# Down projections of six feed-forward stages: some block pairs by seven products in place of eight

## The reference

```python
def swiglu(x, w_in, w_out):                 # first block, D_FF = 4096
    gate, up = jnp.split(x @ w_in, 2, axis=-1)
    return (jax.nn.silu(gate) * up) @ w_out

x = layer_norm(alpha * x + 0.5 * swiglu(x, w_ff1_in[l], w_ff1_out[l]), ln1_g[l], ln1_b[l])
x = layer_norm(alpha * x + mix, ln2_g[l], ln2_b[l])
x = layer_norm(alpha * x + 0.5 * swiglu(x, w_ff2_in[l], w_ff2_out[l]), ln3_g[l], ln3_b[l])

def swiglu_2(h, wg, wu, wd):                # second block, D_FF_2 = 2816
    return (jax.nn.silu(h @ wg) * (h @ wu)) @ wd

x = x + swiglu_2(rms_norm(x, norm_ffn[i]), ffn_gate[i], ffn_up[i], ffn_down[i])
```

## Time and profile before

| | us |
|---|---|
| median of 3 runs | 2325.2 |
| lowest, highest | 2323.91, 2325.67 |
| profiled execution | 2326.54 |
| its span, first to last instruction | 2324.7 |
| TensorE products busy | 2272.9 |
| VectorE busy | 1484.9 |
| ScalarE busy | 1164.6 |
| mean granted clock of TensorE | 0.993 |

### The profile page before, as it was taken

How to read it: one execution, slowest core, us unless ns; L and a number is a source line. 1 busy time by engine, 2 the same in 40 slices (tenths; PEclk the granted TensorE clock), 3 DMA queues, 4 the chain that set the end, 5 groups by cost and what they waited for, 6 DMA issues and landing times.

```text
span 2324.7 us, 33502 instructions
## 1 busy us (share of the span) xinstructions
PE 2272.9 (98%) x13839; PEld 1925.4 (83%) x13839; DVE 1484.9 (64%) x2139; ACT 1164.6 (50%) x1799; POOL 128.8 (6%) x197
## 2 busy tenths in 40 slices
PE   8999999999999999999999999999989999888999
PEld 7888798887888878888898877888878887766887
DVE  5665558857666556665668667666467664565663
ACT  5554346534555435554356344555344554545552
POOL 2100010120000000000100210000000000320000
PEclk9999999999999999999999999999999999999999
DMA  6756474435565556656554446556545665542653
GB/s 224 229 186 214 149 221 126 129 127 189 181 189 191 185 185 201 190 196 202 178 160 137 137 143 204 186 183 215 182 138 180 194 204 169 157 121 90 202 192 133
DMA packets 283561, 408.09 MB, mean 176 GB/s; under 512 B 13701, under 2 KB 170689, under 8 KB 283153
## 3 DMA queue, kind: packets, MB, share of 16 engines
q1 hardware_dynamic: 275600, 380.91, 51.2%
q0 software_dynamic: 7808, 25.04, 3.7%
HBM read 403.98 MB, written 1.91 MB: 175 GB/s over the span
## 4 chain that ended last, share of the span: by engine, by line
PE 86%; DVE 8%; ACT 4%; DMA 1%; issue 1%; POOL 0%; SPq 0%; DVEq 0%; ACTq 0%; POOLq 0%
PE PS L517 24%; PE PS L449 13%; PE PS L451 12%; PE PS L450 12%; PE PS L516 11%; PE PS L446 2%; PE PS L447 2%; PE PS L448 2%; DVE WL L1266 2%; PE PS L519 2%; DVE QX L1513 1%; PE PS L466 1%; ACT WH L922 1%; PE PS L661 0%; ACT PP L978 0%
## 5 line engine op out<-in xcount | busy, mean ns | idle before, releaser
L1266 DVE TENSOR_TENSOR WL<-RW,WH 128x1024 fp32r<-128x1024 f32 (+2 forms) x732 | 870.9, 1221 | 295.4 <-ACT WH L922 292.0
L922 ACT ACTIVATE WH<-RW 128x1024 fp32r<-128x1024 f32 (+2 forms) x732 | 740.4, 1043 | 389.2 <-PE PS L451 217.1
L517 PE MATMUL PS<-XT,WH 128*128 128x512 f32 x2368 | 808.4, 394 | 0.0
L516 PE MATMUL PS<-XT,WL 128*128 128x256 f32 x2072 | 580.5, 280 | 0.0
L517 PEld LDWEIGHTS PS<-XT,WH 128*128 128x128 f32 x2368 | 425.0, 188 | 76.7
L516 PEld LDWEIGHTS PS<-XT,WL 128*128 128x128 f32 x2072 | 390.0, 188 | 13.3
L449 PE MATMUL PS<-WH,HTH 128*128 128x512 f32 x688 | 271.4, 395 | 0.0
L451 PE MATMUL PS<-WH,HTL 128*128 128x512 f32 x688 | 270.8, 394 | 0.0
L450 PE MATMUL PS<-WL,HTH 128*128 128x512 f32 x688 | 269.7, 392 | 0.0
L449 PE MATMUL PS<-WH,XT 128*128 128x512 f32 (+4 forms) x640 | 251.2, 392 | 5.8 <-DVE WL L1266 3.9
L451 PE MATMUL PS<-WH,XT 128*128 128x512 f32 (+4 forms) x640 | 241.8, 378 | 0.0
(11 more groups left out here) (438 smaller groups left out, 2553.3 us busy)
## 6 DMA issues: line engine op xcount, KB each, us to landing
RW<-in_w_ff_in SPq DMA_DIRECT2D x256, 512.0 KB, 4.5
RW<-in_w_ff_out SPq DMA_DIRECT2D x128, 512.0 KB, 4.5
RW<-in_w_in SPq DMA_DIRECT2D x56, 512.0 KB, 4.5
RW<-in_w_gate SPq DMA_DIRECT2D x48, 512.0 KB, 4.1
RW<-in_ffn_gate SPq DMA_DIRECT2D x44, 512.0 KB, 4.5
RW<-in_ffn_up SPq DMA_DIRECT2D x44, 512.0 KB, 4.7
RW<-in_ffn_down SPq DMA_DIRECT2D x44, 512.0 KB, 4.5
RW<-in_w_out SPq DMA_DIRECT2D x16, 512.0 KB, 4.7
```

What stands on the lines that cost most here:

```text
L516: self.e.matmul(k.PS[:, b.n, 0:T], wl, k.XTH[:, kt, :], start=False, stop=False)
L517: ins = self.e.matmul(k.PS[:, b.n, :], wh, k.XT[:, kt, :], start=kt == 0, stop=kt == 7)
L922: self.e.activation(u.hi_out, raw, ACT.Copy).then_inc(*self.s["hi"].up(u.n))
L1266: self.e.tensor_tensor(u.lo_out, raw, u.hi_out.bitcast(F), ALU.subtract).then_inc(*self.s["lo"].up(u.n))
```

## The change

In the down projections five of the sixteen block pairs (contraction tiles 8, 12, 16, 20, 24 and their neighbours), or four of the eleven (6, 10, 12, 16), are computed by Strassen's scheme in Winograd's form. The blocks of the activations are 128 tokens by 128, those of the weights 128 by 256 columns, so a unit is one 2x2 by 2x2 block product. Its products Q1 (a11 b11), Q5, Q6 and Q7 gather in two further banks over all such units of a half, the other three go directly into the banks of the plain products.

- Activations: in the hidden stage VectorE makes S1 to S4 of such a pair (`seven_mix`), ScalarE and VectorE split them (`seven_split`).
- Weights: VectorE makes T1 to T4 from the raw unit (`mix`, four operations of 256 columns, each waiting for the one before), T1 in place of b12, the rest in a buffer MX; then the cut has two copies and two subtractions (1024 and 768 elements) and takes two slots. The sums of the next unit are issued ahead of the cut of a unit.
- Slots: two of XT's parts are lent as slots during the down projection; in the stages of width 4096 the two slots lent before are taken back at the stage's start and lent again after the last such unit of the second half.
- Order: `down` takes the place of `rows`; a unit of seven products is a group of its own. Numbered by contraction tile, the first half of a wide stage is 0 2 | 4 6 | **8** 10 **12** 14 **16** 18 **20** 22 **24** 26 | 28 30, the second 0 2 | 4 6 | **8** **12** 10 **16** **20** 14 **24** 18 | 22 26 28 30 (with six late units: **8** **12** **16** **20** **24** 10 | 14 18 22 26 28 30). In the narrow stages: 0 2 | 4 8 | **6** **10** **12** **16** 14 | 18 20, and 0 2 | 4 | **6** **10** **12** **16** | 8 14 18 20.
- After the last such unit of a half, ScalarE copies Q1 and VectorE brings Q1, Q5, Q6 and Q7 into X with eight operations of 256 columns (`seven_ends`); the residual additions then take X with scale 1.

```diff
+SEVEN = {32: (8, 12, 16, 20, 24), 22: (6, 10, 12, 16)}
+    def seven_part(self, u, kt, hs, bks, qs, x, first, last):
+        k = self.k
+        self.wait_ge("lo", u.n)
+        self.wait_each(x.ready(kt, 0))
+        self.wait_each(hs[2])
...
+        for b, c, (ah, al), (wh, wl), st, sp in ((qs[0], left, a11, b11, first, False), (bks[0], left, a12, b21, False, False),
+                                                 (bks[0], right, s4, b22, False, False), (bks[1], left, a22, t4, False, False),
+                                                 (qs[1], left, s1, t1, first, False), (qs[0], right, s2, t2, False, last),
+                                                 (qs[1], right, s3, t3, False, last)):
+            o = k.PS[:, b.n, c]
+            self.e.matmul(o, ah, wh, start=st, stop=False, skip_group_check=True)
+            self.e.matmul(o, ah, wl, start=False, stop=False, skip_group_check=True)
+            ins = self.e.matmul(o, al, wh, start=False, stop=sp, skip_group_check=True)
...
 class ScalarProgram:
+        if u.seven:
+            self.wait_ge("mix", (u.n, "t4"))
+            self.e.activation(u.hi_out, raw, ACT.Copy).then_inc(*self.s["hi"].up((u.n, "w")))
+            self.e.activation(u.h2, u.mixed.rearrange("p k n -> p (k n)"), ACT.Copy).then_inc(*self.s["hi"].up(u.n))
+            return
+    def seven_ends(self, seq, half, qs, q, scale, x_ready):
+        self.wait_ge("mm", qs[0].full)
+        self.e.activation(q, self.k.PS[:, qs[0].n, 0:256], ACT.Copy).then_inc(*self.s["ffn_a"].up((seq, "q1", half)))
...
 class VectorProgram:
+    def mix(self, u, mixed, free):
...
+        self.e.tensor_tensor(t3, b22, b12, ALU.subtract).then_inc(*up((u.n, "t3")))
+        self.wait_ge("mix", (u.n, "t3"))
+        self.e.tensor_tensor(b12, b12, b11, ALU.subtract).then_inc(*up((u.n, "t1")))
+        self.wait_ge("mix", (u.n, "t1"))
+        self.e.tensor_tensor(t2, b22, b12, ALU.subtract).then_inc(*up((u.n, "t2")))
+        self.wait_ge("mix", (u.n, "t2"))
+        self.e.tensor_tensor(t4, b21, t2, ALU.subtract).then_inc(*up((u.n, "t4")))
...
+    def seven_ends(self, seq, half, qs, q, scale, x_ready):
...
+        self.wait_ge("mm", qs[1].full)
...
+        self.wait_ge("ffn_a", (seq, "q1", half))
+        self.e.scalar_tensor_tensor(out=x11, in0=x11, scalar=scale, in1=q, op0=ALU.mult,
+                                    op1=ALU.add).then_inc(*up((seq, "x11", half)))
+        self.wait_ge("ffn_v", (seq, "x11", half))
+        self.e.tensor_tensor(q, q6, q, ALU.add).then_inc(*up((seq, "q16", half)))
...
+        self.e.tensor_tensor(x22, x22, q, ALU.add).then_inc(*up((seq, "x", half)))
...
 class Walk:
     def cut(self, n):
...
+        u = self.units[n]
+        some = [s for s in self.slots if n < self.xt_until or s[0] not in self.k.xt_slots]
+        if len(some) < (2 if u.seven else 1) or u.seven and self.mix_free is None:
             return
...
+        if n + 1 < len(self.units) and self.units[n + 1].seven and n + 1 in self.loaded and self.mix_free is not None:
+            self.mix(n + 1)
+        self.e.cut(u)
         self.load(n + RAW)
...
+    def down(self, w, nk, half, bks, qs, x, hs, last_n, ends):
...
+            if seven:
+                (k0, u), = held
+                done += 1
+                self.e.seven_part(u, k0, hs[k0], bks, qs, x, done == 1, done == n_s)
+                self.free(u)
+                if done == n_s:
+                    ends(u)
+                yield
+                continue
...
     def out_rows(...):
...
-            e.residual(seq, half, t, bks[t], scale, self.x_done[t])
+            e.residual(seq, half, t, bks[t], 1.0 if hs else scale, [("ffn_v", (seq, "x", half))] if hs else self.x_done[t])
...
     def ffn(...):
+        if nkt == 32:
+            self.end_slots()
...
+            if kt in SEVEN[nkt]:
+                e.seven_mix(f, seq, sl, n)
+                e.seven_split(f, k.HS[nkt][kt], seq, sl, n, ("seven", seq, kt))
+                hs[kt] = (*k.HS[nkt][kt], [("turn_lo", ("seven", seq, kt))])
```

More of the change, by code:

```diff
@@ L2272, in ahead @@
             self.cut(m)
+            if m not in self.cuts:
+                break
     def free(self, u):
[L2275 to L2276 removed]
+        if self.units is not None:
+            self.slots += [(slot, [("mm", u.used)]) for slot in u.slots if self.more or slot not in self.k.more_slots]
     def lend_slots(self, after):
@@ L2383, in tiles, with out_rows @@
                     self.free(u)
+                    self.last_tile = u.used
                 yield
-    def out_rows(self, w, nk, x, scale, ln, order=None, first_n=2):
+    def down(self, w, nk, half, bks, qs, x, hs, last_n, ends):
+        nkt = nk
+        plain = [k0 for k0 in range(0, nk, KU) if k0 not in hs]
+        early, late = plain[:-last_n], plain[-last_n:]
+        groups = [early[:2], early[2:4]]
+        early, sevens = early[4:], list(hs)
+        n_s = len(sevens)
+        for m in range(n_s):
+            groups.append([sevens[m]])
+            more = early[len(early) * m // n_s:len(early) * (m + 1) // n_s]
+            if more:
+                groups.append(more)
+        groups.append(late)
+        first, done = True, 0
+        for group in groups:
+            seven = group[0] in hs
+            held = [(k0, self.take(wsrc(w, k0, KU, 512 * half, 512), nkt if seven else 0)) for k0 in group]
+            if seven:
[7 more added lines that the diff above has]
+                continue
+            for t in range(2):
+                for m, (k0, u) in enumerate(held):
+                    if m == (len(held) - 1 if t == 0 else min(1, len(held) - 1)):
+                        self.late()
+                    self.e.rows_part(u, k0, t, [(0, 512, bks)], x, first and m == 0, group is late and m == len(held) - 1)
+                    if t == 1:
+                        self.free(u)
+                    yield
+            first = False
+    def out_rows(self, w, nk, x, scale, ln, order=None, first_n=2, hs=None):
         e = self.e
@@ L2413, in out_rows @@
         bks = [self.bank(), self.bank()]
-        for n, _ in enumerate(self.rows(w, nk, 512, [(0, 512, bks)], x, order, last_n=last_n)):
+        if hs:
+            qs = [self.bank(), self.bank()]
+            second = self.down(w, nk, 1, bks, qs, x, hs, last_n, ends(1, qs))
+        else:
+            second = self.rows(w, nk, 512, [(0, 512, bks)], x, order, last_n=last_n)
+        for n, _ in enumerate(second):
             if n == parts - last_n - 1:
```

141 lines of the change are left out of this document (122 added, 19 removed).

## The result

The changed kernel takes 2342.0 us, the median of four runs (2339.25 to 2343.2); the kernel before, run beside it, 2325.4 (2323.91 to 2325.78). The ratio is 1.0075, with a 95% interval of 1.0062 to 1.0087: slower, by 16.6 us between the medians. The forecast was 2328 with a range of 2311 to 2341. Slower was the sign that I held a little likelier than faster (0.37 to 0.33), and the size fell 1 us outside the range.

A forecast was written before the change was run, and what follows sets the result against it. Columns streamed by TensorE were taken to bound the down projections. Pairs −16.1, stalls +2, ends +13.2 and clock +4 gave +3.1 us: 2329.6 for the profiled execution, forecast 2328 against the median 2325.2, range 2311 to 2341.

The forecast's parts named there:

- 56 pairs: Down projections: 21 narrow products replace 12 wide ones per block pair, saving 0.288 us each, −16.1 us in all.
- idles at the five transposes: Ends of second halves: late residual of token tile 0 keeps TensorE waiting, +2.8, +2.7, +2.7, +1 and +4, sum +13.2 us.
- stalls inside down projections: TensorE waiting for VectorE in the two short projections, 1 us each, none counted in the long ones: +2 us.
- half clock at the ends: Behind the two longest idles, 3.9 and 4.5 us, the clock falls to 1.2 GHz: +2 each, +4 us.
- The price of a pair on VectorE: Down projections: four sums and two low parts cost VectorE 3.8 us per new pair, against 2.48 us of TensorE.
- my own sign of being wrong: Inside runs of new pairs: TensorE waiting for WL would show that VectorE is the bound; no size given.
- My upper bound of 8: Upper bound in us for TensorE's stalls in down projections, if every unit costs 0.5 more; lower bound 0.
- the idles cost the clock every time: Five transposes: loads of 4.5 us, ends 17.3, clock 10, stalls 4, so +15 us, 2340; chance 0.29.
- The rival on narrow products: Down projections: narrow products to new operands take 0.132 us, so no gain, and the ends make 2344; chance 0.03.
- the ends stay hidden: Ends of halves: fifth cut doesn't wait for its load, no clock falls, −11.7 us, 2313.5; chance 0.32.

The follow-up runs named there:

- The changed kernel once more: The same program as the changed kernel, nothing altered, measured again in the second series of runs: 2342.0 us, ratio 1.0078.
- one held cut: Changed kernel, last of four next-stage weight cuts in second halves issued behind token tile 0's normalization: 2330.7 us; with seven products in long projections only: 2320.2 us.

## Why the prediction was wrong

The sum had the right terms and the right signs; the stalls were sized far too small, and one term was missing. The changed kernel has two profiled executions, its first and the one under "The changed kernel once more", and both are in the table. The transfers are counted from the issue of the write to the first product.

| term | forecast | measured | once more |
|---|---|---|---|
| 56 pairs | −16.1 | −16.8 (0.30 each, from the runs where nothing waits) | −16.8 |
| idles at the five transposes | +13.2 | +14.9 | +16.2 |
| stalls inside down projections | +2 | +7.7 | +8.1 |
| half clock at the ends | +4 | +7.1 (2.2, 1.6, 1.6, 1.7) | +3.5 (1.7, 1.8) |
| transfers of the last mixer | 0 | +3.3 | +2.7 |
| span | +3.1 | +14.5 | +14.7 |

The five measured terms make 16.2, 1.7 over the span's, and 13.7 once more, 1.0 under it. The stretches between the stages also hold differences of both signs (one more fall of the clock in a mixer, a shorter one behind the fourth stage, and 0.4 us of the 2.2 at the first transposes won back a little later).

- **Products: right.** 0.118 us apart. By the estimate from its figures the Trainium skill ("TensorE: Matmul & The Clock Gate", "Back-to-back issue gap") would have made the pairs dearer than what they replace; the runs of one held cut show 0.30 us gained for each.
- **Ends: right in place and mechanism.** 4.18 us of idle where I had 3.9, cut five waiting for a load that could start only after cut one. The third and second came to 2.1 and 2.4 for 2.7, the fourth to 1.6 for 1, the fifth to 5.7 for 4. At the fifth I had VectorE 1.9 us late at the end operations; it was 3.75 (1956.45 to 1960.20), because the cut ahead of them waited for its load: ScalarE stood for 2.18 us, until 1957.97, in front of its copy of that unit.
- **Stalls: the step that failed.** "Unit by unit I get 1 us of stall in each" of the two short stages, and next to none in the long ones. By the table of stretches, with 0.30 per pair, the idles and nothing else, the fourth is 1.3 us longer than that, the fifth 3.2, the sixth 2.9, and the second and third 0.2. Nearly all of it lies in the runs of new pairs. Four pairs without a stall take 9.9 us; in the fifth the run of the first half took 10.7 and that of the second 12.3 (1944.11 to 1956.45 below), in the sixth 10.6 and 12.2. In the fourth the run of five lost 0.5 us, as I had allowed, and a plain unit behind it 0.8 (at 1683.30, where TensorE waits for a WL). The price of a pair on VectorE was right, 3.91 us for 3.8. Timeline of VectorE after, one pair in the fifth:
```profile
1914.54 0.42 DVE L1321 TENSOR_TENSOR MX<-RW 128x256 f32<-128x256 f32 x1
1915.00 0.42 DVE L1323 TENSOR_TENSOR RW<-RW 128x256 f32<-128x256 f32 x1
...
1915.92 0.43 DVE L1327 TENSOR_TENSOR MX<-RW,MX 128x256 f32<-128x256 f32 x1
1916.26 1.22 DVE L1333 TENSOR_TENSOR WL<-RW,WH 128x1024 fp32r<-128x1024 f32 x1
1917.40 0.95 DVE L1336 TENSOR_TENSOR WL<-MX,WH 128x768 fp32r<-128x768 f32 x1
1918.45 0.42 DVE L1321 TENSOR_TENSOR MX<-RW 128x256 f32<-128x256 f32 x1
```
  and TensorE in the second half of the same stage:
```profile
1944.11 0.28 PE L534 MATMUL PS<-XT,HTH 128*128 128x256 f32 x1
1947.45 0.39 PE L534 MATMUL PS<-WH,HTH 128*128 128x256 f32 x1 [0.67 <-DVE WL L1336]
1951.36 0.39 PE L534 MATMUL PS<-WH,HTH 128*128 128x256 f32 x1 [1.16 <-DVE WL L1336]
1956.45 0.39 PE L461 MATMUL PS<-WH,HTH 128*128 128x512 f32 x1
```
  The two that wait are 3.91 us apart: TensorE has taken on VectorE's pace. It was my own sign of being wrong, TensorE waiting for WL inside the runs of new pairs. What was off was how late VectorE is when the run begins, which I had worked out along one chain, without the ends of the first half and the waits for loads in front of it. In the fifth ScalarE's last copy ahead of the ends of the first half waited for a load until 1929.29, so VectorE began these ends at 1931.52, 4 us behind the last product of the run (1927.31), and the first sums of the second half at 1935.83. My upper bound of 8 for the term is near the measured 7.7 by luck: it stood for 0.5 us more in every unit, and the first three long stages have next to no stall.
- **Clock: too small in one execution, right in the other.** I charged the two longest idles and let the 2.7 us ones go. In the first profiled execution the idles of 2.40 and 2.06 us were followed by the lower level too. In the second they were not (2.33 and 2.10), only the first and the fifth cost time, 3.5 us, close to the 4 that I had, and the span is the same. Windows of that execution at the second and fourth transposes (at the third, 1124.20 to 1126.20, the clock was 1.00 too):
```profile
853.80:855.80 2.00, 2.00 (x12) 1.70 (x13) 1.94 (x3) 0.60 (x1) 0.00 (x0) 1.00 0.00 0
1695.60:1697.60 2.00, 1.96 (x8) 1.70 (x9) 2.00 (x3) 1.36 (x2) 0.00 (x0) 0.62 0.00 0
```
  The clock fell at the fourth, behind 2.58 us, and nearly all that it cost went into a wait for weights which was there anyway.
- **Missing: the transfers of the mixer.** No step touched them. They show as the longer wait of TensorE there, 7.0 us for 3.0.

The rival "the idles cost the clock every time", 2340, came closest, and for its own reasons only half: the ends cost 14.9 where it had 17.3, the clock 7.1 where it had 10 (3.5 in the second execution), and the stalls 7.7 where it had 4; that the sum comes near is luck in part, with 3.3 us in it that no rival had. The rival on narrow products, 2344, was as near, and the distance of 0.118 us refutes it. The rival "the ends stay hidden" is refuted for the program as it stands, and the run with one cut held shows how near it was: one cut that VectorE begins at 280.66 in place of 275.63 brings three of the five idles back to those of before.

Shown by runs are: that the pairs save 0.30 us each, that three ends hang on the fifth cut, that the short stages lose nothing with two spaced pairs in a half in place of four in a row, and that a held cut is paid elsewhere, some 0.5 us at each of three stages for the first and 1.1 more for the second. Whether the number of pairs or their spacing matters in the short stages, and what sets the level of the ZC transfers, wasn't separated.

## What to carry to other kernels

A trade of TensorE's columns for VectorE's work is decided where VectorE's in-order queue meets something that TensorE waits for, not by busy shares: list, behind each instruction that now waits, all that the queue holds up to the next result TensorE needs, the loads that are chained to it included. Optional work that was issued early because the engine had time should be moved behind that result, one piece at a time, since each piece reappears at the next place where somebody waits. And spread the dear pieces so that each has its cheap neighbours, and take fewer where there are few neighbours: the same scheme stalled for 3 us in a stage with four in a row and kept its whole saving with two apart (number and spacing changed together).

## What the runs showed of the hardware

- In the changed kernel the granted clock was 0.50 behind an idle of 2.40 us, fell to 0.50 about 1 us behind the end of one of 2.06, and stayed at 1.00 behind one of 2.51. In the second execution of the same program it stayed at 1.00 behind 2.33 and 2.10 and fell behind 2.58 (0.62 over the next 2 us). So near 2 to 2.6 us the length of the idle alone doesn't tell. Nor does the place: in a mixer between the third and fourth stages TensorE waits once for the same result, 2.10 us before and 2.06 after; the clock behind it was 1.00 before (1237.80 to 1242.80) and 0.74 after (1240 to 1245).
- Chained operations of 256 elements on VectorE start 0.46 us apart, unchained ones 0.34 (1915.92 to 1916.26): 0.12 for a wait, as in the earlier trace rows.
- The same write of 288 KB to memory, issued at the same distance from the weight loads, made GpSimd's next transfer wait 2.3 to 3.4 us in the profiled executions of some programs and 4.4 to 4.9 in those of others; the changed kernel was on the slower level in both of its own.
